# The place of w_down_2's weight pieces inside their ring slots: from 16 and 80 bytes past a multiple of 128 to 0

## The reference, cut to what matters

```python
D_FF_2 = 5632
def conv_gated_mlp(h, w_up, conv_w, conv_b, w_down):
    up = h @ w_up                                   # (256, 2048) @ (2048, 11264)
    up = causal_depthwise_conv(up, conv_w) + conv_b
    gate, val = jnp.split(up, 2, axis=-1)
    return (jax.nn.silu(gate) * val) @ w_down       # (256, 5632) @ (5632, 2048)
# in second_block:
    f = conv_gated_mlp(h, w_up[l], conv_ffn_w[l], conv_ffn_bias[l], w_down[l])
    x = x + rms_norm(f, norm_ffn_post[l])
```

## The kernel before

| tile | starts at, modulo 128 | used in the split products as |
|---|---|---|
| whi, every slot | 16 | stationary in the feature form, moving in the token form |
| wlo, every slot | 80 | the same |
| xh, xl | 32 | moving (w_down_2's last two pieces) |
| hh, hl, ch, cl, mh, ml, oh, ol, yfh, yfl | 32 | moving in the feature form; hh, hl, ch, cl also stationary in the token form, in the first block |
| dh, dl | 0 | stationary in the token form, w_down_2 |
| hf (plain float32, L352) | 32 | moving, against raw (stationary) at 0 |

## Time and profile before

### The profile page before, as it was taken

How to read it: one execution, slowest core, us unless ns; L and a number is a source line. 1 busy time by engine, 2 the same in 40 slices (tenths; PEclk the granted TensorE clock), 3 DMA queues, 4 the chain that set the end, 5 groups by cost and what they waited for, 6 DMA issues and landing times.

```text
span 2584.7 us, 42715 instructions
## 1 busy us (share of the span) xinstructions
PE 2533.3 (98%) x18976; PEld 2379.1 (92%) x18976; DVE 1669.4 (65%) x2016; ACT 1141.4 (44%) x1311; POOL 11.2 (0%) x24
## 2 busy tenths in 40 slices
PE   6999999999998999999999999999999999999998
PEld 3688799999998999999999999999899889988997
DVE  5366666677787755555545579776667557764775
ACT  3422555544445434434434552054445444443554
POOL 0000000000000000000000000000000000000000
PEclk8999999999999999999999999999999999999999
DMA  9966565587875755555555555455455555555543
GB/s 401 371 241 231 213 225 198 212 300 289 303 288 195 289 184 196 184 192 194 184 193 193 183 181 178 147 180 177 149 181 196 195 182 193 192 184 194 186 175 128
DMA packets 77224, 547.90 MB, mean 212 GB/s; under 512 B 8848, under 2 KB 8976, under 8 KB 12272
## 3 DMA queue, kind: packets, MB, share of 16 engines
q1 hardware_dynamic: 74304, 533.53, 56.9%
q0 software_dynamic: 2448, 11.14, 1.1%
q10 hardware_dynamic: 288, 0.50, 0.1%
HBM read 539.90 MB, written 5.24 MB: 211 GB/s over the span
## 4 chain that ended last, share of the span: by engine, by line
PE 96%; DMA 1%; DVE 1%; ACT 1%; issue 1%; SPq 0%; DVEq 0%; ACTq 0%
PE acc L295 23%; PE acc L299 23%; PE acc L297 23%; PE acc L315 5%; PE acc L316 5%; PE acc L317 5%; PE acc L352 4%; DMA raw<-in_w_mod 1%; PE mp L382 1%; PE mp L315 1%; PE mp L317 1%; PE mp L316 1%; PE mp L441 0%; DVE macc L426 0%; PE mp L1857 0%
## 5 line engine op out<-in xcount | busy, mean ns | idle before, releaser
L263 DVE TENSOR_TENSOR wlo<-raw,whi 128x1024 fp32r<-128x1024 f32 x779 | 942.3, 1223 | 679.4 <-ACT whi L254 678.1
L254 ACT ACTIVATE whi<-raw 128x1024 fp32r<-128x1024 f32 x779 | 818.3, 1058 | 1180.9 <-PE acc L299 881.3
L295 PE MATMUL acc<-hh,whi 128*128 128x256 f32 x3360 | 940.1, 280 | 5.5 <-issue 5.5
L299 PE MATMUL acc<-hl,whi 128*128 128x256 f32 x3360 | 941.6, 280 | 0.0
L297 PE MATMUL acc<-hh,wlo 128*128 128x256 f32 x3360 | 934.7, 278 | 0.0
L295 PEld LDWEIGHTS acc<-hh,whi 128*128 128x128 f32 x3360 | 635.5, 189 | 10.6 <-issue 8.9
L299 PEld LDWEIGHTS acc<-hl,whi 128*128 128x128 f32 x3360 | 632.0, 188 | 0.0
L297 PEld LDWEIGHTS acc<-hh,wlo 128*128 128x128 f32 x3360 | 630.3, 188 | 0.5
L299 PE MATMUL acc<-ml,whi 128*128 128x256 f32 x1536 | 430.4, 280 | 0.0
L295 PE MATMUL acc<-mh,whi 128*128 128x256 f32 x1536 | 426.6, 278 | 0.0
L297 PE MATMUL acc<-mh,wlo 128*128 128x256 f32 x1536 | 426.5, 278 | 0.0
(11 more groups left out here) (332 smaller groups left out, 2213.1 us busy)
## 6 DMA issues: line engine op xcount, KB each, us to landing
raw<-in_w_in SPq DMA_DIRECT2D x98, 1024.0 KB, 4.9
raw<-in_w_mod SPq DMA_DIRECT2D x96, 1024.0 KB, 5.7
raw<-in_w_up SPq DMA_DIRECT2D x88, 1024.0 KB, 4.8
raw<-in_w_mlp_in SPq DMA_DIRECT2D x64, 1024.0 KB, 4.8
raw<-in_w_mlp_out SPq DMA_DIRECT2D x64, 1024.0 KB, 4.8
raw<-in_w_down SPq DMA_DIRECT2D x44, 1024.0 KB, 4.8
raw<-in_w_out SPq DMA_DIRECT2D x32, 1024.0 KB, 4.9
raw<-in_w_fourier_out SPq DMA_DIRECT2D x8, 1024.0 KB, 5.5
```

Of the source, the lines that this page charges most:

```text
L254: nc.scalar.activation(ring(whi, xh, st.p), raw_slot(k)[:, 2 * GC * j:2 * GC * (j + 1)], ACT.Copy)\
L263: nc.vector.tensor_tensor(ring(wlo, xl, st.p), raw_slot(k)[:, 2 * GC * j:2 * GC * (j + 1)], ring(whi, xh, st.p).bitcast(f32), ALU.subtract ...
L295: nc.tensor.matmul(dst, whi[:, r, cols], hi[:, kt, :], start=begin, stop=False, skip_group_check=True)
L299: last = nc.tensor.matmul(dst, whi[:, r, cols], lo[:, kt, :], start=False, stop=kt == nkt - 1, skip_group_check=True)
```

## The change

whi and wlo become flat tiles of four slots 4224 bytes (33 x 128) apart. The tiles now both begin at a multiple of 128. A piece starts 16 bytes (whi) or 80 bytes (wlo) into its slot, so that it is at 16 or 80 modulo 128 as before; but a piece of w_down_2 (the set DOWN) starts at the slot's own start, a multiple of 128. To make room, region_a loses 384 bytes, and fss becomes a view of the first 24 numbers of fixed. hold_yN grows by 96 bytes, which puts xh and xl at 0 modulo 128. Tiles made after wlo move by 896 bytes, those after region_a by 512; both are multiples of 128, so their place modulo 128 stays. Every read of a piece goes through two new functions in place of ring. The instructions are the same in kind, number and order.

```diff
+PITCH = 2 * GC + 32
+HI_AT, LO_AT = 4, 20
+DOWN = set()
+for behind, count in ((0, 24), (24 + 48, 32), (24 + 48 + 32 + 64, 32)):
+    DOWN.update(range(len(PIECE) - behind - count, len(PIECE) - behind))
...
-        whi = sb("whi", [P, 8 * GC + 16], f32r)[:, 4:8 * GC + 4].rearrange("p (r n) -> p r n", r=4)
-        wlo = sb("wlo", [P, 8 * GC + 16], f32r)[:, 4:8 * GC + 4].rearrange("p (r n) -> p r n", r=4)
+        whi = sb("whi", [P, 4 * PITCH], f32r)
+        wlo = sb("wlo", [P, 4 * PITCH], f32r)
...
-            "region_a", 32768 + 512,
+            "region_a", 32768 + 128,
...
-            [("hold_yN", [P, 2, D], f32), ("xh", [P, 2, 2 * GC], f32r), ("xl", [P, 2, 2 * GC], f32r)])
-        fss = sb("fss", [P, 3, 2, 4])
+            [("hold_yN", [P, 2 * D + 24], f32), ("xh", [P, 2, 2 * GC], f32r), ("xl", [P, 2, 2 * GC], f32r)])
+        fss = fixed[:, :, :].rearrange("p g t -> p (g t)")[:, 0:24].rearrange("p (a t g) -> p a t g", a=3, t=2)
...
-        def ring(part, extra, p):
-
-            last = p - len(PIECE) + 2
-            return extra[:, last, :] if last >= 0 else part[:, p % 4, :]
+        def ring_hi(p):
+
+            if p >= len(PIECE) - 2:
+                return xh[:, p - len(PIECE) + 2, :]
+            at = p % 4 * PITCH + (0 if p in DOWN else HI_AT)
+            return whi[:, at:at + 2 * GC]
+
+        def ring_lo(p):
+
+            if p >= len(PIECE) - 2:
+                return xl[:, p - len(PIECE) + 2, :]
+            at = p % 4 * PITCH + (0 if p in DOWN else LO_AT)
+            return wlo[:, at:at + 2 * GC]
...
-            r = st.p % 4
+            wh, wl = ring_hi(st.p), ring_lo(st.p)
...
-                    nc.tensor.matmul(dst, hi[:, kt, t0:t0 + P], whi[:, r, cols], start=kt == 0, stop=False)
+                    nc.tensor.matmul(dst, hi[:, kt, t0:t0 + P], wh[:, cols], start=kt == 0, stop=False)
```

More of the change, by code:

```diff
@@ L253, in hi_piece @@
                 act.wait_ge(S["used"], st.p - 3)
-            nc.scalar.activation(ring(whi, xh, st.p), raw_slot(k)[:, 2 * GC * j:2 * GC * (j + 1)], ACT.Copy)\
+            nc.scalar.activation(ring_hi(st.p), raw_slot(k)[:, 2 * GC * j:2 * GC * (j + 1)], ACT.Copy)\
                 .then_inc(S["hi_n"], 1)
@@ L262, in lo_piece @@
             dve.wait_ge(S["hi_n"], st.p + 1)
-            nc.vector.tensor_tensor(ring(wlo, xl, st.p), raw_slot(k)[:, 2 * GC * j:2 * GC * (j + 1)],
-                                    ring(whi, xh, st.p).bitcast(f32), ALU.subtract).then_inc(S["lo_n"], 1)
+            nc.vector.tensor_tensor(ring_lo(st.p), raw_slot(k)[:, 2 * GC * j:2 * GC * (j + 1)],
+                                    ring_hi(st.p).bitcast(f32), ALU.subtract).then_inc(S["lo_n"], 1)
             st.p += 1
@@ L294, in feature_piece @@
                     begin = kt == 0 and t % 2 == 0
-                    nc.tensor.matmul(dst, whi[:, r, cols], hi[:, kt, :], start=begin, stop=False,
+                    nc.tensor.matmul(dst, wh[:, cols], hi[:, kt, :], start=begin, stop=False,
                                      skip_group_check=True)
-                    nc.tensor.matmul(dst, wlo[:, r, cols], hi[:, kt, :], start=False, stop=False,
+                    nc.tensor.matmul(dst, wl[:, cols], hi[:, kt, :], start=False, stop=False,
                                      skip_group_check=True)
-                    last = nc.tensor.matmul(dst, whi[:, r, cols], lo[:, kt, :], start=False,
+                    last = nc.tensor.matmul(dst, wh[:, cols], lo[:, kt, :], start=False,
                                             stop=kt == nkt - 1, skip_group_check=True)
@@ L314, in token_piece @@
                     dst = bank[:, off:off + GC]
-                    nc.tensor.matmul(dst, hi[:, kt, t0:t0 + P], whi[:, r, cols], start=kt == 0, stop=False)
-                    nc.tensor.matmul(dst, hi[:, kt, t0:t0 + P], wlo[:, r, cols], start=False, stop=False)
-                    last = nc.tensor.matmul(dst, lo[:, kt, t0:t0 + P], whi[:, r, cols], start=False,
+                    nc.tensor.matmul(dst, hi[:, kt, t0:t0 + P], wh[:, cols], start=kt == 0, stop=False)
+                    nc.tensor.matmul(dst, hi[:, kt, t0:t0 + P], wl[:, cols], start=False, stop=False)
+                    last = nc.tensor.matmul(dst, lo[:, kt, t0:t0 + P], wh[:, cols], start=False,
                                             stop=kt == nkt - 1)
@@ L366, in mm_lr @@
                     dst = acc[i][0:LRW, x * GC:x * GC + NT]
-                    nc.tensor.matmul(dst, whi[:, r, cols], hi[:, kt, :], start=kt == 0, stop=False)
-                    nc.tensor.matmul(dst, whi[:, r, cols], lo[:, kt, :], start=False, stop=False)
-                    last = nc.tensor.matmul(dst, wlo[:, r, cols], hi[:, kt, :], start=False, stop=kt == KT - 1)
+                    nc.tensor.matmul(dst, wh[:, cols], hi[:, kt, :], start=kt == 0, stop=False)
+                    nc.tensor.matmul(dst, wh[:, cols], lo[:, kt, :], start=False, stop=False)
+                    last = nc.tensor.matmul(dst, wl[:, cols], hi[:, kt, :], start=False, stop=kt == KT - 1)
             last.then_inc(S["used"], 1)
@@ L2050, in _ @@
                         pe.wait_ge(S["lo_n"], st.p + n + 1)
-                    wh, wl = ring(whi, xh, st.p + n), ring(wlo, xl, st.p + n)
+                    wh, wl = ring_hi(st.p + n), ring_lo(st.p + n)
                     for k in range(2):
```

## The result

The changed kernel takes 2610.98 us (median of 4 runs, 2609.93 to 2612.08), the kernel before 2583.24 us (4 runs, 2582.26 to 2583.86). The ratio is 1.0098, 95% interval 1.0086 to 1.011. The prediction was 2582 us, range 2570 to 2591. The kernel became slower where a time 1 us under the old one was forecast, and the measured time lies outside the range.

What follows compares the result with a forecast made beforehand. TensorE's streaming rate was taken to bound the kernel. All terms summed to 0 on 2586.47 us profiled, 2583.0 in timed runs; a small gain being likelier than a loss, the forecast was 2582.0 us, range 2570 to 2591.

Steps and rivals of the forecast that it cites:

- The step that failed: Feature-form matmuls, 14,688 in all: slots and tiles at new places modulo 256 and 512 were costed at 0.
- the 0.35 ns: Feature-form matmuls: 0.35 ns each, either way, would already make 5.2 us, the limit for telling a change from none.
- rival 3: 14,688 feature matmuls at new places modulo 256 and 512: 0.35 to 0.7 ns each, 5 to 10 us, either sign; chance 0.07.
- The stream's own excess: Split matmuls stream 16.8 ns slower per 512 columns than plain data; over w_down_2's 1056 this bounds -17.7 to +17.7 us.
- Show one steady rate: Argument against a feature-form effect: ring slots and column offsets in multiples of 512 bytes show 115.6 ns over 177.52 us.
- Moving a row from 16 or 80 to 32 gained nothing: w_down_2's moving rows: xh, xl at 32 took 234.5 ns, whi, wlo at 16, 80 took 232.5; if anything 2 ns lost.
- w_down_2, taken as 0: Moving rows of w_down_2's 1056 matmuls go to 0 modulo 128: no effect expected on their 232.6 ns.
- the forecast's band of 227.7 to 237.5: Time in ns of a w_down_2 matmul; leaving this band would prove the forecast wrong.
- Rival 2: w_down_2: both streams on one residue get in each other's way, 8.4 ns a matmul, +8.9 us, up to +17.7; chance 0.14.
- The reading of the bottleneck: Whole kernel: TensorE, busy 2533.3 of 2584.7 us, bounds; in the long stretches nothing waits for data.
- the conversions: ScalarE's copies (1060 ns) and VectorE's subtractions (1225 ns): the output's residue does nothing, 0 us.
- the tail: Behind the last matmul, about 8.2 us of VectorE, ScalarE and the store: unchanged.

Runs made afterwards that it cites:

- e2: Kernel before with only the ring's pitch changed to 4224 bytes, tiles used in split products kept in place modulo 256: 2612.78 us, ratio 1.0108.
- e1: Kernel before with only the tiles behind the ring moved to the changed kernel's places, ring untouched at pitch 4096: 2628.36 us, ratio 1.0162.
- e7: Kernel before with the tiles behind the ring moved to the changed kernel's places and the ring moved along by 128 bytes: 2589.05 us, ratio 1.0013.
- The sweeps: Kernel before with the ring's places modulo 256 changed stage by stage within one run; totals not comparable, w_down_2 pieces took 2720 to 2840 ns.

## Why the prediction was wrong

- **The step that failed:** "All other pieces keep their residue modulo 128, but slot by slot they get other residues modulo 256 and 512 ... I cost it at 0". It measured +50 ns a feature piece, 2.1 ns a matmul, six times the 0.35 ns that I named as decisive. e2 shows the pitch alone gives it, e1 the shift alone gives more, e7 that undoing the relative shift takes it back. This was rival 3, with a chance of 0.07 and a price of 5 to 10 us.
- **Its bound was not made.** I had written that nothing in the trace varies these residues, and then priced the term by what would "already make 5.2 us". The stream's own excess was there as a bound, as for w_down_2: a feature matmul takes 115.6 ns where half of L352's 215.8 is 107.9, so 7.7 ns each way over 14,688 of them, more than 100 us. An unknown with that exposure had to widen the range. The argument against it, that column offsets of multiples of 512 show one rate, says nothing on 128.
- **"Show one steady rate"** was read from the second round of w_up_2, 115.6 ns a matmul. The first round, in the same trace, ran at 117.8 (152.64 us for 54 pieces). The rows at hand already held a second rate of the size that was then measured, 2.2 ns a matmul, and it was not looked for.
- **"Moving a row from 16 or 80 to 32 gained nothing"** compared xh with whi, where dh was at 0 for both; three places of the moving rows out of an unknown pattern do not show that it is flat. The sweeps found 2720 to 2840 ns a piece of w_down_2.
- **w_down_2, taken as 0:** 232.6 became 230.3 ns, -2.4 us on 1056. That this lies inside the forecast's band of 227.7 to 237.5 is luck: the 0 stood for no effect of the places, and there is one, -56 ns a piece in two slots and none in the other two. What counts is the relation to dh, not the multiple of 128: pieces at 128 and 0 are both multiples of 128, and with dh at 128 the first take 2735 ns, the second 2792.
- **Rival 2** (both streams on one residue are slower) has the wrong sign for the token form, 2720 with all on one, and the right one for the feature form, 2880 at (160,160), where it was not looked for. The Trainium skill's independent read ports ("TensorE: Matmul & The Clock Gate", Part 2, "Step-by-step: what each phase is for") would make both 0. The measurements decide: the time of the pair depends on where the two lie.
- **The reading of the bottleneck, the waits, the conversions and the tail** held: VectorE and ScalarE kept their times, and all of the loss is in TensorE's rate.

Open: why these places fit or clash; no run isolates a mechanism. Open too is what makes a stretch enter one rhythm or the other.

## What to carry to other kernels

When a change moves a buffer, compare the places of all operands of the bounding engine before and after, modulo at least 256 bytes, also those of tiles merely allocated behind it, and choose pads and pitches that keep them; price the edit by the number of instructions whose relative addresses it changes. Where rates are at stake, sweep the places stage by stage in one run, and test the winner in the whole kernel, since the same places can run at two rates. Before calling a rate steady, read it from every stage that has the same instructions.

## What the runs showed of the hardware

At the full granted clock (2.4 GHz), a split-form matmul takes 113.3 to 122.2 ns for 256 columns (2720 to 2933 ns a piece), with the same instructions and only the places of the operands changed; the lowest, 2720 ns a piece, was reached in both forms. Plain f32 matmuls did not react to the one move that they saw: the 384 of L352 in the earlier trace rows take 82.87 us, and in the changed kernel (L368), with hf at 32 and no longer at 160 modulo 256 and raw where it was:

```profile
1597.88:1680.76 82.88, 82.88 (x386) 72.96 (x385) 70.23 (x184) 1.69 (x2) 0.00 (x0) 1.00 0.45 158
```

The same few rates come back to the nanosecond from stage to stage and run to run (2720, 2773, 2800, 2827, 2880 and some between). One pair of places can hold two of them: (144,208) 2773 and 2827, (224,224) 2720 and 2827, both with hh at 160. Once entered, a rate was held over 54 to 64 pieces.
